# Naming ScalarE's table of logarithm and exponential at four places

## What is computed

```
def rmsnorm(x, g):
    y = x * rsqrt(mean(x * x, -1) + EPS);  return y * g

# first block
x   = x + 0.5 * m2 * swiglu(modulate(rmsnorm(x, norm_ffn1), m0, m1), ...)
px  = modulate(rmsnorm(x, norm_mix), m3, m4) @ w_mix_in
q, k, v, gb, gc, u = split_heads(px, q_norm, k_norm)      # rmsnorm of q and k per head
a   = softmax attention over context and latents;  sc = gb * short_conv3(gc * u)
x   = x + m5 * (concat(rmsnorm(a), rmsnorm(sc)) @ w_mix_out)
x   = x + 0.5 * m8 * swiglu(modulate(rmsnorm(x, norm_ffn2), m6, m7), ...)
x   = rmsnorm(x, final_norm)
# second block
la  = log_sigmoid(lr @ gk_up + gk_bias) / 16              # decay, four tiles
ret = head_rmsnorm(o_rf + flip(o_rb)) * silu(rg)          # four heads
gla = head_rmsnorm(o_gf + flip(o_gb)) * silu(gg)          # four heads
x   = x + g1 * (concat(ret, gla) @ w_out)
x   = x + g2 * peer_ffn(modulate(rmsnorm(x, norm2_w), ...))   # gather, gelu, softmax
return rmsnorm(x, norm_f_w)
```

## Time and profile before

| | us |
|---|---|
| median of 3 runs | 3331.07 |
| lowest, highest | 3330.17, 3332.3 |
| the profiled execution | 3331.79 |
| its span, first to last instruction | 3330.0 |
| TensorE, busy | 2835.7 |
| VectorE, busy | 1695.3 |
| GpSimd, busy | 1076.2 |
| ScalarE, busy | 950.0 |
| of it table loads, 124 | 159.1 |

### The profile page before, as it was taken

One profiled execution on the slowest core, in us unless ns is written; L12 is line 12 of the kernel. 1 busy time (PEld: TensorE's weight loads), 2 busy tenths in 40 slices (PEclk: granted clock), 3 DMA queues, 4 the chain that ended last, 5 costly groups with the idle time before them and its releaser, 6 DMA issues.

```text
span 3330.0 us, 30025 instructions
## 1 busy us (share of the span) xinstructions
PE 2835.7 (85%) x11064; PEld 1914.3 (57%) x11064; DVE 1695.3 (51%) x3686; ACT 950.0 (29%) x1732; POOL 1076.2 (32%) x731
## 2 busy tenths in 40 slices
PE   6999999989988999979984688998877777787776
PEld 4999989966456887858832565554322233333222
DVE  3666750024534622030054436776777667767765
ACT  3111131144333223142224333333322222222221
POOL 1222222132013444322210025554544444444442
PEclk8999999989999999989986799999999999999999
DMA  4555521111003522312110028999999999999997
GB/s 194 173 174 183 176 79 59 60 63 63 0 26 124 192 101 90 93 38 69 53 39 1 7 64 339 385 409 427 425 427 427 427 427 427 427 427 427 427 427 298
DMA packets 126958, 722.13 MB, mean 217 GB/s; under 512 B 15204, under 2 KB 17516, under 8 KB 60140
## 3 DMA queue, kind: packets, MB, share of 16 engines
q0 software_dynamic: 73728, 536.90, 38.6%
q1 hardware_dynamic: 37448, 127.67, 11.1%
q10 hardware_dynamic: 15652, 55.90, 5.4%
HBM read 718.31 MB, written 2.10 MB: 216 GB/s over the span
## 4 chain that ended last, share of the span: by engine, by line
PE 57%; DMA 25%; DVE 9%; ACT 5%; issue 3%; POOL 1%; SPq 0%; DVEq 0%; ACTq 0%; POOLq 0%
PE acc L540 14%; PE acc L541 14%; PE acc L542 13%; DMA arena<-in_peer_rows,squares 7%; DMA wring<-in_peer_rows,squares 6%; DMA hid<-in_peer_rows,squares 6%; PE sums L974 4%; PE acc L974 3%; DMA resid<-in_peer_rows,squares 2%; DMA modw<-in_peer_rows,squares 2%; PE sums L481 2%; PE misc L481 1%; DVE hid L1589 1%; ACT L1036 1%; DVE hid_parts L1595 1%
## 5 line engine op out<-in xcount | busy, mean ns | idle before, releaser
L2279 POOL TENSOR_TENSOR wring_parts<-wring,wring_parts 128x1024 fp32r<-128x1024 f32 (+1 forms) x215 | 513.2, 2399 | 1519.4 <-ACT wring_parts L1036 1519.2
L540 PE MATMUL acc<-hid_parts,wring_parts 128*128 128x384 f32 (+1 forms) x2128 | 792.4, 372 | 84.2 <-DVE hid_parts L1595 64.1
L542 PE MATMUL acc<-hid_parts,wring_parts 128*128 128x384 f32 (+1 forms) x2128 | 770.8, 362 | 0.0
L541 PE MATMUL acc<-hid_parts,wring_parts 128*128 128x384 f32 (+2 forms) x1696 | 615.1, 363 | 0.0
L540 PEld LDWEIGHTS acc<-hid_parts,wring_parts 128*128 128x128 f32 x2128 | 404.3, 190 | 160.5 <-issue 71.2
L542 PEld LDWEIGHTS acc<-hid_parts,wring_parts 128*128 128x128 f32 x2128 | 405.0, 190 | 38.3
L1036 ACT ACTIVATE wring_parts<-wring 128x1024 fp32r<-128x1024 f32 (+1 forms) x215 | 222.1, 1040 | 625.3 <-DMA wring<-in_w_ffn_out 222.4
L541 PEld LDWEIGHTS acc<-hid_parts,wring_parts 128*128 128x128 f32 (+1 forms) x1696 | 323.1, 191 | 31.6 <-issue 3.8
L1036 ACT ACTIVATE hid<-hid 128x2 f32<-128x2 f32 (+2 forms) x292 | 65.6, 224 | 762.4 <-DVE arena L2114 238.3
L2291 POOL DMA_INDIRECT arena<-in_peer_rows,squares x180 | 202.7, 1126 | 243.5 <-PE acc L974 155.2
L2291 POOL DMA_INDIRECT wring<-in_peer_rows,squares x158 | 174.5, 1105 | 216.0 <-PE acc L974 158.8
(11 more groups left out here) (357 smaller groups left out, 4355.1 us busy)
## 6 DMA issues: line engine op xcount, KB each, us to landing
wring<-in_w_ffn_in SPq DMA_DIRECT2D x88, 512.0 KB, 6.0
modw<-in_w_ada ACTq DMA_DIRECT2D x56, 512.0 KB, 4.0
modw<-in_w_mod ACTq DMA_DIRECT2D x48, 512.0 KB, 3.9
wring<-in_w_ffn_out SPq DMA_DIRECT2D x32, 512.0 KB, 3.5
wring<-in_w_in SPq DMA_DIRECT2D x28, 512.0 KB, 3.5
wring<-in_w_mix_in SPq DMA_DIRECT2D x18, 512.0 KB, 3.5
wring<-in_peer_w_q SPq DMA_DIRECT2D x16, 512.0 KB, 5.6
hid<-in_w_ada SPq DMA_DIRECT2D x6, 1024.0 KB, 17.5
```

Source lines behind the costliest of these rows:

```text
L540: nc.tensor.matmul(o, wh, high, start=first, stop=False)
L541: nc.tensor.matmul(o, wh, low, start=False, stop=False)
L542: return nc.tensor.matmul(o, wl, high, start=False, stop=last)
L2279: nc.gpsimd.tensor_tensor(Wlor[:, p, 0:blocks, 0:cols], Wlo[:, p, 0:blocks, 0:cols], Whir[:, p, 0:blocks, 0:cols], ALU.subtract).then_inc( ...
```

## The change

A function `logs_and_exponentials` is added to ScalarE's program. It issues one load of the table set `natural_log_exp_and_others`, which holds both functions (and the square, the copy and the absolute value). It is called ahead of the first statistics, ahead of the statistics behind each of the two FFN output products, and behind the last gate of the second block's projection. Nothing else in the text of the program differs, and the other engines' instructions are the same.

```diff
+            def logs_and_exponentials():
+
+                nc.scalar.preload_act_table_set("natural_log_exp_and_others")
...
+            logs_and_exponentials()
             emptied(act, UNIT["tokens"] + 4)
             emptied(act, UNIT["tokens"] + 5)
             stat(KD, TC, lambda j: x_[:, j, :])
...
             s0 = TILE_OF["mix_in"]
+            logs_and_exponentials()
             stat(KD, TC, lambda j: behind_chunks("ffn1_out", j, TC), meanwhile=range(s0, s0 + W_RING), only=1)
...
             ff_parts("ffn2_out", UNIT["ffn2_in"], ff512, hi_ff512)
+            logs_and_exponentials()
             stat(KD, T, lambda j: behind_chunks("ffn2_out", j, T))
...
                 if t == 0:
                     ahead(s0 + 24)
+            logs_and_exponentials()
```

## The result

| | median us | runs |
|---|---|---|
| before | 3333.14 | 6 runs, 3330.17 to 3337.80 |
| after | 3309.94 | 6 runs, 3305.72 to 3313.15 |

The ratio is 0.9928, 95% interval 0.9915 to 0.9941: 23.2 us faster (19.7 to 28.3 by the interval), where 20.8 were forecast. The forecast of 3310.2 is 0.3 from the measured median. Part of that is luck: the forecast started from a median of 3331.07 for before, and the three runs of it taken later lie higher (3333.14 over all six), so the differences are 2.4 apart where the times are 0.3 apart. The sum was not right term by term either, and the second half of this document is about that.

The account below looks back on a forecast made before the run. TensorE (57%) and DMA (25%) hold the chain, ScalarE only 5%, so only waited-for loads count. Terms 1.28 - 2.74 - 1.3 - 9.03 - 5.16 - 3.87 = -20.8 took 3331.79 to 3311.0, median 3310.2; range 3300 to 3317.

Parts of the forecast that it names:

- One load costs what its row says: Any removed load that is waited for: gives 1.29 to 1.30 us, with no drain of about 1.38 us added.
- Place 1, +1.28: First statistics: the new load stands ahead of the first square, so TensorE starts 1.28 us later and nothing comes back.
- Attention's start, -1.37: Load pair at 813: the first is beside TensorE's sums, worth 0.08 us; the second is waited for, worth 1.29.
- Attention's end, -1.37: Load pair at 963: same form as the pair at attention's start, so 1.37 us saved.
- Four pairs ahead of modulated norms, -0.3 each: At 671, 1024, 1439, 1961: rstd 2.58 us earlier, but VectorE and GpSimd share a port in turns; 1.3 us in all.
- The rival that VectorE is not held up: At the four modulated norms each pair is worth its full 2.58 us, 10.3 in place of 1.3: 3301.2 us; chance 0.14.
- Final norm of the first block, 0: Two removed loads give nothing, since VectorE's copies, not ScalarE's rstd, are already last.
- Decay -9.03, retention heads -5.16: Seven decay loads at 1.29 us, ScalarE still setting the pace; in four retention heads only the exponential's load counts.
- the rival of a risen clock: In the heads TensorE stays at 2.4 GHz, seven sums 0.96 us shorter, 6.7 more gained: 3303.5 us; chance 0.10.
- The rival of slow retention products: In the decay rounds TensorE's products at the lower clock become the bound, seven loads worth nothing: 3319.2 us; chance 0.10.
- Gated heads, -3.87: Four gated heads: three exponential loads are waited for, 1.29 us each; the fourth is beside the output projection.
- The slower case: First FFN: longer TensorE idle time lets the lower clock reach into the products; 40 us of it give 3350; chance 0.03.

Follow-up runs that it names:

- the moved name: The changed kernel with its first named load moved behind the second square of the first statistics: 3309.13 us, ratio 0.9931 to before.
- the kernel with the fourth name alone: The kernel before with the table named only behind the last gate of the second block's projection: 3308.92 us, ratio 0.9934.
- the two variants of before in which GpSimd was held back or relieved: Before with GpSimd waiting for normalised tiles at four norms, 3326.59 us; before with 16 weight-tile subtractions replaced by zero fills, 3325.09 us.
- the kernels with replaced subtractions: Before and after with GpSimd's subtractions of 16 weight tiles near four modulated norms replaced by zero fills: 3325.09 and 3292.72 us.
- one wait on GpSimd: GpSimd waits before the third weight tile at four modulated norms until the normalised tiles are there: added to after 3289.05 us, to before 3326.59 us.

## Why the prediction was right, and where it was not

**The kernel is bound by TensorE and the gathers, and only loads that another engine waits for count.** Held. 45 loads fewer gave 23 us, and of 25 plus 24 removed loads, the 25 gave 21.9 and the 24 gave 3.1.

**One load costs what its row says.** Held: 1.28 per load in the heads with an additional load, 2.56 per decay round with two loads. The Trainium skill, page "ScalarE: Activation LUTs", section "What ACT_TABLE_LOAD costs", puts a drain of 1.38 us beside each load; by it the time would have come out near 3288 (an estimate from that page). The measurement is 3309.94, and the traces disagree with the rule: 0.01 us stand ahead of a load and 0.02 between it and the activation behind it.

**Place 1, +1.28.** The mechanism held (the load at 28.35 stands ahead of the square). The size was too small: the sums start 1.4 later by the traces of the moved name, and the first result behind them comes 1.9 later, since the sums took 12.79 and not 12.28. The medians of the moved name give 0.8, which the runs can't tell from nothing.

**Attention's start, -1.37.** Held. From the square (812.41 before, 813.53 after) to the softmax's exponential (816.87, 816.62) it is 4.46 and 3.09. TensorE's work behind it gained more than that in the first pair of traces, 2.3, and 0.9 in the second.

**Attention's end, -1.37: this step failed.** The saving itself is there: the exponential starts 0.72 behind the logarithm and not 2.00. But the sum takes TensorE's work around it as unchanged, and that became longer by more. TensorE's sums, the first load, a weight load of the sums and the first residual sum, in before and then in after:

```profile
960.36 3.89 PE L481 MATMUL sums<-squares,cst 128*128 128x512 f32 x8 [3.42 <-ACT squares L1036]
961.32 0.19 PEld L481 LDWEIGHTS sums<-squares,cst 128*128 128x128 f32 x1 [0.24 <-issue]
963.08 1.28 ACT L1036 ACT_TABLE_LOAD   x1
...
973.53 0.75 DVE L1818 SCALAR_TENSOR_TENSOR resid<-acc,mods,resid 128x512 f32<-128x512 f32 x1 [1.34 <-PE acc L542]
```

```profile
959.19 5.40 PE L481 MATMUL sums<-squares,cst 128*128 128x512 f32 x8 [3.42 <-ACT squares L1036]
960.28 0.34 PEld L481 LDWEIGHTS sums<-squares,cst 128*128 128x128 f32 x1 [0.36 <-issue]
...
974.05 0.75 DVE L1826 SCALAR_TENSOR_TENSOR resid<-acc,mods,resid 128x512 f32<-128x512 f32 x1 [2.89 <-PE acc L542]
```

The stretch from 940 to 975, and TensorE's products in it, in before and in after:

```profile
940.00:975.00 35.00, 25.37 (x89) 12.92 (x89) 13.14 (x23) 15.60 (x27) 0.00 (x0) 1.00 0.01 2
971.47 0.40 PE L541 MATMUL acc<-arena_parts,wring_parts 128*128 128x512 f32 x1
```

```profile
940.00:975.00 35.00, 27.37 (x84) 13.90 (x83) 12.34 (x21) 12.35 (x22) 0.00 (x0) 0.90 0.00 1
971.44 0.63 PE L540 MATMUL acc<-arena_parts,wring_parts 128*128 128x512 f32 x1
```

The granted clock was 1.00 before and 0.90 after, and the lower of the two levels shows twice: the sums take 5.40 in place of 3.89, and single products that took 0.40 take 0.63, so that the first residual sum comes 8.03 behind VectorE's L1782 and not 6.48. From the first square (959.69 and 958.53) to that residual sum there are 13.84 us before and 15.52 after, 13.83 and 16.55 in the second traces. The term was worth +1.7 and +2.7 instead of -1.37.

All nine traces in which the loads of this place are gone show it (7.99 to 8.05 behind L1782, sums of 5.40 or 6.47). The second trace of before and the kernel with the fourth name alone do not (6.47 and 6.49, sums of 3.89). It does not follow from the loads of this place, though: the first slow weight load, at 960.28, is 1.75 us behind the first square, and the first of the two loads stood 3.39 behind it in before. And the two variants of before in which GpSimd was held back or relieved have 8.92 and 7.95 with both loads in place. What these have in common with after is that something had shifted earlier in the kernel. Why the level falls here with them and not in before is open.

**Four pairs ahead of modulated norms, -0.3 each.** The mechanism held, the size was too small. rstd comes 2.7 earlier, by two loads and what is around them. From rstd to the products it then takes 2.0, 2.2, 2.0 and 2.5 longer (the table's rows for after, less those for before), so that 0.7, about 0.5, 0.7 and 0.2 are left, 2.1 in all instead of 1.3. Counted from the last square, as the prediction asked, the products start 0.70 earlier at the first and third, over the 0.5 that it allowed, and 0.21 at the last; at 1024, where ScalarE waits for weight tiles in between, it is 1.55 in the first pair of traces and 0.34 in the second. The rival that VectorE is not held up expected 10.3; the kernels with replaced subtractions show what takes the 8.7 us that are missing. VectorE's first operations were to take "about 2.8" each between GpSimd's: two took 5.32. The prediction also had GpSimd pushed back by as much as VectorE ran; its four took 9.71 and not 9.25, so VectorE did most of the waiting.

**Final norm of the first block, 0.** Held: from the last residual sum of the second FFN to L1836 there are 5.84 and 5.85. The sums for the next norm behind it are among the stretches that scatter.

**Decay -9.03, retention heads -5.16.** From the first absolute value to the scan there are 50.41 us before, 35.38 after: 15.0 against 14.2. The rounds are 3.68 where 3.66 was forecast. The other 0.8 is one head: its sums took 1.13 and not 2.08, the upper clock level for once. So the rival of a risen clock came true for one head of seven, in both traces of after; with the moved name it did for none, and in the second trace of before this head has 1.55. The rival of slow retention products did not come: from 1743 to 1760 the granted clock was 1.00.

**Gated heads, -3.87.** The heads are 4.55 apart and not 5.84 (1879.28 less 1874.73 in ScalarE's timeline for after), 3.87 for three, as forecast. The stretch ahead of them lost 1.2 (87.8 us before from the scan to the first head's sums, 88.95 after), but the two variants of before with GpSimd held back or relieved lose 1.9 and 1.1 there too, so it is not shown to be the names'. The projection behind the heads won 1.25. Two stretches of 10 us from its start, in before and in after:

```profile
1902.00:1912.00 10.00, 10.00 (x31) 7.30 (x31) 4.02 (x6) 4.63 (x6) 0.00 (x0) 0.72 0.01 2
```

```profile
1882.00:1892.00 10.00, 10.00 (x36) 7.45 (x37) 4.11 (x7) 2.47 (x4) 0.00 (x0) 0.85 0.10 29
```

TensorE is busy throughout in both; at a granted clock of 0.85 in place of 0.72 it gets through 36 matmuls and not 31.

**The experts move as one block.** Held within what can be seen: the two traces of the first comparison differ by 2.7 us there, and second traces of one kernel by 5.3.

**The sum.** VectorE runs the same operations in the same order in both kernels, so each start can be subtracted from that of its counterpart. The table gives how much this lead or lag changes over a stretch, after less before (minus is faster), in the two pairs of traces; places are those of the first trace of before.

| stretch | forecast | first pair | second pair |
|---|---|---|---|
| first norm and first FFN, 23 to 665 | +1.28 | +2.3 | +0.8 (a late weight tile in both) |
| norm near 671 | -0.3 | -0.7 | -0.7 |
| attention's start, 800 to 860 | -1.37 | -2.3 | -0.9 |
| attention's end, 949 to 974 | -1.37 | +1.7 | +2.7 |
| norm near 1024, 1012 to 1040 | -0.3 | -1.5 | -0.3 |
| second FFN, 1040 to 1416 | 0 | -0.6 | -1.3 |
| final norm to projection, 1416 to 1615 | -0.3 | -0.6 | -3.8 |
| decay and retention heads, 1740 to 1796 | -14.2 | -15.0 | -16.0 |
| from there to the gated heads, to 1883 | 0 | +1.1 | +1.4 |
| gated heads and projection, to 1951 | -3.87 | -5.1 | -5.0 |
| norm near 1961 | -0.3 | -0.2 | -0.2 |

With small rests between the stretches these make 20.6 and 23.2 us when the experts begin (the first pair is 21.4 apart there, with 0.8 from conditioning that came earlier). At the end of the span the first pair is 18.7 apart; by the medians it is 23.2. The forecast's 20.8 holds one term that was wrong by 3 to 4 (attention's end), and several that came out up to 3.5 better than forecast. The large terms, decay and heads, were right in mechanism and nearly in size; that the others cancelled so closely is luck.

**The slower case** did not come: at the end of the first FFN after is only 1.6 us behind before (2.3 with the conditioning that came earlier), where 20.8 would have eaten the gain.

## What to carry to other kernels

Before removing a wait on one engine, look at what another engine does meanwhile on a resource that the released engine needs: here the loads were worth 3 us at places where ScalarE got 31 us back, and one wait on GpSimd then gave some 18 to 21 us that alone gave only 5. Take each removed load at its row's duration where it stands between two waiting engines and at zero elsewhere, and put a named load beside work of the engine behind it, not ahead of it (1.4 to 1.9 us in the traces here, though the medians can't show it). Compare at least two traces of each kernel before giving a difference of 1 to 3 us at one stage to the change.

## What the runs showed of the hardware that was not expected

- Contention costs more than the overlap suggests. Two VectorE operations of 0.75 us took 5.32 beside GpSimd's subtractions of 2.3 us, four of them 6.38; with GpSimd silent, the two took 1.42. An operation of VectorE can stand for a whole subtraction, also in before, where 7.0 us over four norms were lost that the prediction had not counted.
- A fill by GpSimd of 0.95 us per tile beside the norm left VectorE's pair at 1.41; here the fills were over before VectorE began.
- A change on another engine went with other stretches at TensorE's lower level: at the attention's end its sums took 5.40 and not 3.89 and its products 0.63 and not 0.40 for 3 us, while at the projection the clock was 0.85 and not 0.72. Both repeated in the second trace of after. What brings the level down at one place and not at the other is not shown.
- One late piece of the modulation weights costs 4 to 6 us, in 2 of 14 traces.
